# Prompt attention of a hybrid decoder: groups of four tiles formed across block ends, query blocks in alternating order, one VectorE write per group

## The chip, the cores and the metric

The kernel runs on one core of one Trainium2 chip. The metric is the device time of one execution in microseconds (us). Three executions of the kernel before took 3279.99, 3284.44 and 3284.48 us; their median is 3284.44 us.

## What is computed

The program is one inference step of a two-layer decoder for a prompt of 1024 tokens and eight sample tokens that share the weights. Layer 0 is a recurrent block (a gated linear recurrence) with a feed-forward network; layer 1 is sparse attention with a feed-forward network. The change touches only the prompt's attention in layer 1. Its part of the reference is this, with 16 query heads in 4 groups, head width 64 and 1024 query positions in 8 blocks of 128:

```
s_s = einsum(qs, k_g) * scale;  p_s = masked_softmax(s_s, m_s);  o_s = einsum(p_s, v_g)   # selected blocks
s_w = einsum(qs, kw) * scale;   p_w = masked_softmax(s_w, m_w);  o_w = einsum(p_w, vw)    # window of 512
o = g[..., 0:1] * o_c + g[..., 1:2] * o_s + g[..., 2:3] * o_w
```

The compressed branch `o_c` is finished before the stage in question starts; it stands in `oc`, and the other two branches are added to it.

## The kernel before

**Blocks, units and tiles.** A block is one pair of heads (one head in each half of the 128 partitions), given by `r` and `t`, and one query block `i` of 128 positions. `BLOCKS` (L1166) lists 4 x 2 x 8 = 64 of them, and the innermost index is `i` from 0 to 7. Each block has two units, one for each branch `b`: the selected branch reads key tiles 0 to `i`, the window branch key tiles `max(0, i-4)` to `i` (`branch_tiles`, L1169). A tile is 128 queries by 128 keys, for both heads. The eight blocks of one head pair have 2, 4, 6, 8, 10, 11, 12 and 13 tiles, 66 together; the stage has 528 tiles.

**Groups.** Tiles are handled in groups of at most four, since a half of a score bank holds 512 columns. L1185 cuts the tiles of one block into fours, and what is left at the end of a block is a group of its own: a head pair has 1+1+2+2+3+3+3+4 = 19 groups, the stage 152. Of these 112 have four tiles, 8 three, 24 two and 8 one. The rest of the text numbers groups by `g`.

**A ring of scores.** Masked scores are kept in `ring[half]`, 32 tiles each. A unit needs neighbouring places there (`SLOT`), since ScalarE and GpSimd handle a unit in one instruction for each half.

**Steps.** Every engine runs a list written out in the same order of steps `s`. In step `s` group `s` enters and group `s - LAG`, with `LAG` = 5, leaves:

- TensorE (`att_pe`, L1207) transposes the probabilities of group `s-5` (L1235), computes the scores of group `s` (L1220) and multiplies group `s-6` by the values (L1248). Scores have two buffers, so `scores(g)` waits until VectorE has finished the maxima of group `g-2`. `transposes(g)` waits for `p_ready` of the unit to which the last tile of the group belongs. The first `values` of a block waits for `oc_added` of the block two before, which used the same accumulator.
- VectorE (`att_dve`, L1295) does, in this order, a reciprocal for each unit that ended two steps before (L1335), the copy of the transposed upper queries if `s-5` is even (L1323), the addition of a finished block into `oc` (L1329), and `maxima(s)`: for each half a one-element write `dmark` (L1304), then one masked reduction for each run (L1312 with the selection mask, L1315 with the triangular one), each with an accumulator read and a drain. A run is a stretch of tiles of one unit inside a group; the diagonal tile of the selected branch is a run of its own. A run that starts a unit begins from a constant, one that continues a unit begins from the running maximum `nmx`.
- ScalarE (`att_act`, L1267) copies the transposed lower queries of group `s-5` (L1273), for odd groups the upper queries too (L1277), and then takes the exponentials of the units that ended in group `s-1`, one instruction for each half (L1284).
- GpSimd (`att_pool`, L1358) scales each unit by gate and reciprocal, one instruction for each half (L1368), and so sets `p_ready`.

Nothing plans this at run time: the order is fixed by these lists, and the engines meet through semaphores. The sample stage (`smp_pe`, L1386) waits for all 64 `oc_added`; so do the loads of its second sample and later ones.

Of the kernel before, what the change touches and what calls it, by code (L numbers as in the profile page):

```python
# [13 lines left out]
P = 128  # L14
# [70 lines left out]
def build(nc, a, o):  # L85
# [1079 lines left out]

    BLOCKS = [(r, t, i) for r in range(4) for t in range(2) for i in range(QT)]  # L1166
    LAG = 5
# [3 lines left out]

    GROUPS, LAST_GROUP, FIRST_GROUP, UNIT_END, SLOT, EVICTED = [], [], [], [], [], []
    _pos, _owner = 0, [None] * RING
    for _j, (_r, _t, _i) in enumerate(BLOCKS):
        _tiles = []
        for _b in range(2):
            _kt = branch_tiles(_i, _b)
            if _pos + len(_kt) > RING:
                _pos = 0
            SLOT.append(_pos)  # L1180
            _tiles += [(_b, _k, _pos + _n) for _n, _k in enumerate(_kt)]
            _pos += len(_kt)
            UNIT_END.append(None)
        FIRST_GROUP.append(len(GROUPS))
        for _p in range(0, len(_tiles), 4):  # L1185
            _g = _tiles[_p:_p + 4]
            EVICTED.append(max([_owner[_x] + 1 for _, _, _x in _g if _owner[_x] is not None], default=0))
            for _b, _k, _x in _g:
                _owner[_x] = len(GROUPS)
                UNIT_END[2 * _j + _b] = len(GROUPS)  # L1190
            GROUPS.append((_j, _g))
        LAST_GROUP.append(len(GROUPS) - 1)
    NG = len(GROUPS)
    NU = 2 * len(BLOCKS)

    def runs(g, split_diagonal):
        j, tiles = GROUPS[g]
        i = BLOCKS[j][2]
        out = []
        for n, (b, k, x) in enumerate(tiles):  # L1200
            if out and out[-1][0] == b and not (split_diagonal and b == 0 and k == i):
                out[-1][4] += 1
            else:
                out.append([b, k, x, n, 1])
        return out

    def att_pe(pe):  # L1207
# [6 lines left out]
        def scores(g):  # L1214
            r, t, i = BLOCKS[GROUPS[g][0]]
            after(pe, sem("max_done"), 2 * (g - 1))
            for b, k, x, n, w in runs(g, False):
                for half in range(2):
                    hs = slice(64 * half, 64 * half + 64)
                    mm = pe.matmul(PS[half][:, g % 2, n * P:(n + w) * P], QR[hs, r + 4 * t, i * P:(i + 1) * P],  # L1220
                                   KH[b][hs, t, k * P:(k + w) * P], start=True, stop=True, skip_group_check=True)
            mm.then_inc(sem("s_done"), 1)

        def transposes(g):
            j, tiles = GROUPS[g]
            pe.wait_ge(sem("p_ready"), 2 * (2 * j + tiles[-1][0]) + 2)
            after(pe, sem("pt0_ready"), g)
            after(pe, sem("pt_even_ready"), (g + 1) // 2)
            after(pe, sem("pt_odd_ready"), g // 2)
            for half in range(2):  # L1230
                for n, (b, k, x) in enumerate(tiles):
                    for e in range(2):
# [6 lines left out]
        def values(g):  # L1239
            j, tiles = GROUPS[g]  # L1240
            r, t, i = BLOCKS[j]
            if g == FIRST_GROUP[j]:
                after(pe, sem("oc_added"), j - 1)
            pe.wait_ge(sem("pt0_ready"), g + 1)
            pe.wait_ge(sem("pt_odd_ready" if g % 2 else "pt_even_ready"), g // 2 + 1)
            for n, (b, k, x) in enumerate(tiles):
                for half in range(2):
                    mm = pe.matmul(PS[j % 2][64 * half:64 * half + 64, 2, 0:P],  # L1248
                                   VT[b][:, k, t * P + 64 * half:t * P + 64 * half + 64],
                                   pt[g % 2][:, half, n * P:(n + 1) * P], start=(b == 0 and k == 0),  # L1250
                                   stop=(b == 1 and k == i), skip_group_check=True)
# [10 lines left out]
    def half_rows(g, e):  # L1262
        n = len(GROUPS[g][1])
        to = pt[g % 2][:, :, 0:n * P].rearrange("p h (n q) -> p h n q", q=P)[:, :, :, 64 * e:64 * e + 64]
# [30 lines left out]
    def att_dve(dve):  # L1295
        def maxima(g):
            j, tiles = GROUPS[g]
            r, t, i = BLOCKS[j]
            dve.wait_ge(sem("s_done"), g + 1)
            for half in range(2):  # L1300
                if half == 0:
                    after(dve, sem("t0_done"), EVICTED[g])
                    after(dve, sem("t1_done"), EVICTED[g])
                dve.memset(dmark, 0.0)  # L1304
                for b, k, x, n, w in runs(g, True):
                    ps, pb = PS[half][:, g % 2, n * P:(n + w) * P], ring[half][:, x * P:(x + w) * P]
# [18 lines left out]
        def add(j):  # L1325
            r, t, i = BLOCKS[j]
            dve.wait_ge(sem("pv_done"), LAST_GROUP[j] + 1)
            dst = OC[:, r + 4 * t, i * P:(i + 1) * P]
            dve.tensor_tensor(dst, dst, PS[j % 2][:, 2, 0:P], ALU.add).then_inc(sem("oc_added"), 1)  # L1329

        for s in range(NG + LAG + 2):
# [4 lines left out]
            if 0 <= s - LAG < NG and (s - LAG) % 2 == 0:  # L1336
                copy_out(s - LAG)
            if s - LAG - 2 in LAST_GROUP:
                add(LAST_GROUP.index(s - LAG - 2))
            if s < NG:  # L1340
# [1312 lines left out]
```

## Time and profile before

| what | value |
|---|---|
| median of three runs | 3284.44 us (3279.99 to 3284.48) |
| span of the profiled execution | 3282.0 us |
| TensorE busy over the span | 3120.2 us (95%) |
| VectorE busy over the span | 2003.9 us (61%) |
| ScalarE busy | 836.5 us (25%) |
| GpSimd busy | 1187.7 us (36%) |
| prompt attention, first masked reduction to last value matmul | 1706.6 to 2104.6 us |

The profiled execution has a span of 3282.0 us, and the median of the runs is 2.4 us above it. A busy share over the whole span says little here, because TensorE carries the large matrix products of the other stages; what a change in prompt attention is worth is read in its own window of 398 us. "issue" names idle time in which the engine waited for nothing that the profile shows; in this stage such a gap often hides a wait for a semaphore, as can be seen from what the other engines do at that moment.

### The profile page before, as it was taken

To read this page: it belongs to the slowest core of one execution; us is meant where nothing else is said; L and a number is where in the kernel's file an instruction comes from. 1 tells how busy PE (TensorE), PEld (TensorE's weight loads), DVE (VectorE), ACT (ScalarE), POOL (GpSimd) and SP (SyncE) were. 2 spreads that over 40 slices of the span, in tenths; PEclk is the share of its full clock that TensorE was granted. 3 is DMA by queue.
4 is the path that set the end of the run, shared out by engine and by line. 5 is a ranking of instruction groups with operands and counts; after the bars stand their busy time and mean duration, and the time that the engine had idled before them with its cause. 6 is when DMAs were issued, how large, how long until landed. Compare 5 with 4: busy or idle time off the path is not lost.

```text
span 3282.0 us, 57052 instructions
## 1 busy us (share of the span) xinstructions
PE 3120.2 (95%) x22560; PEld 2835.1 (86%) x22560; DVE 2003.9 (61%) x3712; ACT 836.5 (25%) x1404; POOL 1187.7 (36%) x801
## 2 busy tenths in 40 slices
PE   6999999999999999999889999998999999999996
PEld 4988989999999998999656666675989999999996
DVE  4567286657475676764468888501259567585776
ACT  4555131101010102110237777400231101010001
POOL 1332424444434443334025555300424444444441
PEclk8999999999999999999869999999999999999998
DMA  5223322122121112321662000274221111111112
GB/s 201 83 67 102 127 102 91 65 72 83 59 96 52 65 46 94 130 78 39 206 213 104 2 2 2 74 243 159 103 96 40 51 46 46 46 46 47 51 46 113
DMA packets 78015, 277.89 MB, mean 85 GB/s; under 512 B 8858, under 2 KB 19362, under 8 KB 74546
## 3 DMA queue, kind: packets, MB, share of 16 engines
q1 hardware_dynamic: 75202, 256.83, 23.0%
q10 hardware_dynamic: 2576, 17.73, 1.6%
q8 instruction: 170, 2.79, 0.3%
q14 instruction: 67, 0.55, 0.1%
HBM read 247.54 MB, written 36.27 MB: 86 GB/s over the span
## 4 chain that ended last, share of the span: by engine, by line
PE 76%; DVE 10%; issue 7%; ACT 3%; DVEq 2%; DMA 1%; SPq 0%; POOL 0%; POOLq 0%; ACTq 0%
PE PB L2008 32%; PE PA L2008 30%; PE PB L1413 3%; DVE ring L1315 3%; DVE ring L1312 1%; PE PA L2044 1%; PE PA L1382 1%; PE PB L2044 1%; ACT ring L1284 1%; DVEq L1316 1%; DMA mw<-in_mw 1%; PE PC L284 1%; DVE pt L1323 1%; PE PC L1235 1%; PE PB L1452 0%
## 5 line engine op out<-in xcount | busy, mean ns | idle before, releaser
L1780 POOL TENSOR_TENSOR w_hi<-w_raw,misc 128x1024 fp32r<-128x1024 f32 x192 | 378.1, 1969 | 1535.5 <-PE PA L2008 635.8
L1782 POOL TENSOR_TENSOR w_lo<-w_raw,w_hi 128x1024 fp32r<-128x1024 f32 x192 | 560.3, 2918 | 27.3
L2008 PE MATMUL PA<-hB_hi,w_hi 128*128 128x348 f32 x1272 | 274.1, 324 | 0.0
L2008 PE MATMUL PB<-hB_hi,w_hi 128*128 128x348 f32 x1272 | 272.3, 322 | 0.0
L2008 PE MATMUL PA<-hB_hi,w_lo 128*128 128x348 f32 x1272 | 271.6, 322 | 0.0
L2008 PE MATMUL PB<-hB_hi,w_lo 128*128 128x348 f32 x1272 | 271.5, 322 | 0.0
L2008 PE MATMUL PA<-hB_lo,w_hi 128*128 128x348 f32 x1272 | 271.2, 321 | 0.0
L2008 PE MATMUL PB<-hB_lo,w_hi 128*128 128x348 f32 x1272 | 271.0, 321 | 0.0
L2008 PEld LDWEIGHTS PA<-hB_lo,w_hi 128*128 128x128 f32 x1272 | 215.4, 188 | 0.0
L2008 PEld LDWEIGHTS PB<-hB_hi,w_hi 128*128 128x128 f32 x1272 | 214.9, 188 | 0.4
L2008 PEld LDWEIGHTS PB<-hB_lo,w_hi 128*128 128x128 f32 x1272 | 215.1, 188 | 0.0
L2008 PEld LDWEIGHTS PA<-hB_hi,w_hi 128*128 128x128 f32 x1272 | 214.4, 188 | 0.4
L2008 PEld LDWEIGHTS PA<-hB_hi,w_lo 128*128 128x128 f32 x1272 | 214.4, 188 | 0.0
L2008 PEld LDWEIGHTS PB<-hB_hi,w_lo 128*128 128x128 f32 x1272 | 214.1, 188 | 0.0
L1368 POOL TENSOR_SCALAR ring<-ring,gtok,psm 128x640 f32<-128x640 f32 (+7 forms) x256 | 196.5, 772 | 0.1
L1284 ACT ACTIVATE ring<-ring,nmx 128x640 f32<-128x640 f32 (+7 forms) x256 | 185.8, 731 | 11.4 <-DVE nmx L1315 10.4
L486 DVE TENSOR_TENSOR ua<-ua,rms 128x1032 f32<-128x1032 f32 x48 | 114.3, 2382 | 67.5 <-ACT ua L424 67.2
L486 DVE TENSOR_TENSOR ub<-ub,rms 128x1032 f32<-128x1032 f32 x46 | 85.9, 1867 | 86.0 <-ACT ub L424 86.0
L1235 PEld LDWEIGHTS PC<-ident,ring 64*128 64x128 f32 x1056 | 77.3, 138 | 64.8 <-issue 43.7
L374 DVE TENSOR_TENSOR t<-t,sq 128x1032 f32<-128x1032 f32 x28 | 48.7, 1738 | 136.4 <-ACT sq L368 135.1
L537 DVE TENSOR_TENSOR O<-O,PB 128x1032 f32<-128x1032 f32 x40 | 49.1, 1228 | 134.0 <-PE PB L2008 133.2
L1235 PE MATMUL PC<-ident,ring 64*128 64x64 f32 x1056 | 96.3, 228 | 34.5 <-DVE pt L1323 26.2
(640 smaller groups left out, 6897.5 us busy)
## 6 DMA issues: line engine op xcount, KB each, us to landing
w_raw<-in_w SPq DMA_DIRECT2D x196, 512.0 KB, 3.6
mt<-in_mw SPq DMA_DIRECT2D x32, 1024.0 KB, 5.0
pages<-in_pages SPq DMA_DIRECT2D x64, 384.0 KB, 4.2
x_dram<-X SPq DMA_DIRECT2D x12, 1032.0 KB, 4.0
X<-x_dram SPq DMA_DIRECT2D x3, 4128.0 KB, 12.4
mw<-in_mw SPq DMA_DIRECT2D x4, 2048.0 KB, 22.8
mt_even<-in_mw SPq DMA_DIRECT2D x8, 1024.0 KB, 5.0
mt_odd<-in_mw SPq DMA_DIRECT2D x8, 1024.0 KB, 5.4
```

What stands on the lines that cost most here:

```text
L374: dve.tensor_tensor(acc, acc, sq_of(n, k), ALU.add).then_inc(sem("acc_added"), 1)
L486: dve.tensor_tensor(u[:, 2:2 + TOK], u[:, 2:2 + TOK], rms, ALU.mult)
L537: dve.tensor_tensor(dst, dst, ps, ALU.add).then_inc(sem("sum_out"), 1)
L1235: mm = pe.transpose(PCD[e][:, c:c + 64], ring[half][q, x * P:(x + 1) * P], ident[q, q])
L1284: act.activation(p, p, ACT.Exp, bias=nmx[:, u % 16, half:half + 1], scale=-1.0, accum_out=psm[:, u % 16, half:half + 1]).then_inc(sem("exp ...
L1315: mx = dve.tensor_tensor_reduce(pb, ps, wmask[:, c0:c0 + w * P], -SCALE, first, ALU.add, ALU.min, nm)
L1368: pool.tensor_scalar(p, p, gtok[:, i, gate:gate + 1], psm[:, u % 16, half:half + 1], ALU.mult, ALU.mult).then_inc(sem("p_ready"), 1)
L1413: mm = pe.matmul(dst.rearrange("p g (j b) -> p j g b", b=8), (sw1k if kv == 0 else sw1v)[:, m, :], rhs, start=(m == 0), stop=(m == 15), sk ...
L1780: pool.tensor_tensor(hi, raw, zero.broadcast_to([P, 1024]), ALU.add)
L1782: pool.tensor_tensor(lo, raw, hi.bitcast(F32), ALU.subtract).then_inc(sem("w_split"), 1)
L2008: mm = pe.matmul(PS[ps][:, c, 0:width], w[:, w0:w0 + P], x[:, k, c * width:(c + 1) * width], start=(k == 0 and n == 0), stop=(k == K - 1 a ...
L2044: mm = pe.matmul(PS[(p0 + b) % 2][:, c, 0:CW], w[(t + b) % 2][:, k * P:(k + 1) * P], x[:, k, c * CW:(c + 1) * CW], start=(first and i == 0 ...
```

## The change

Three things change in prompt attention.

1. The order of the eight query blocks inside a head pair is 7, 3, 6, 2, 5, 1, 4, 0 in place of 0 to 7.
2. The tiles of all blocks are put in one list and cut into fours, so a group may hold the end of one block and the start of the next: 132 groups, all of four tiles. `GROUPS`, `UNIT_END`, `LAST_GROUP` and `EVICTED` are worked out for it, and `runs` keeps the block beside the branch. `values` now waits for `oc_added` in every group, for the block two before the one of the group's last tile, which may have ended in the group just before.
3. The one-element write `dmark` is made once in a group in place of once for each half.

```diff
--- before.py
+++ after.py
@@ -1163,46 +1163,43 @@
             act.dma_start(QR[64 * h:64 * h + 16, 4 * t:4 * t + 4, :],
                           q_dram[2][t * P:(t + 1) * P].rearrange("(n h d) c -> h d n c", h=2, d=16)[h]).then_inc(sem("q_back"), 16)
 
-    BLOCKS = [(r, t, i) for r in range(4) for t in range(2) for i in range(QT)]
+    BLOCKS = [(r, t, i) for r in range(4) for t in range(2) for i in (7, 3, 6, 2, 5, 1, 4, 0)]
     LAG = 5
 
     def branch_tiles(i, b):
         return list(range(0 if b == 0 else max(0, i - 4), i + 1))
 
-    GROUPS, LAST_GROUP, FIRST_GROUP, UNIT_END, SLOT, EVICTED = [], [], [], [], [], []
-    _pos, _owner = 0, [None] * RING
+    TILES, UNIT_END, SLOT = [], [], []
+    _pos = 0
     for _j, (_r, _t, _i) in enumerate(BLOCKS):
-        _tiles = []
         for _b in range(2):
             _kt = branch_tiles(_i, _b)
             if _pos + len(_kt) > RING:
                 _pos = 0
             SLOT.append(_pos)
-            _tiles += [(_b, _k, _pos + _n) for _n, _k in enumerate(_kt)]
+            TILES += [(_j, _b, _k, _pos + _n) for _n, _k in enumerate(_kt)]
             _pos += len(_kt)
-            UNIT_END.append(None)
-        FIRST_GROUP.append(len(GROUPS))
-        for _p in range(0, len(_tiles), 4):
-            _g = _tiles[_p:_p + 4]
-            EVICTED.append(max([_owner[_x] + 1 for _, _, _x in _g if _owner[_x] is not None], default=0))
-            for _b, _k, _x in _g:
-                _owner[_x] = len(GROUPS)
-                UNIT_END[2 * _j + _b] = len(GROUPS)
-            GROUPS.append((_j, _g))
-        LAST_GROUP.append(len(GROUPS) - 1)
+            UNIT_END.append((len(TILES) - 1) // 4)
+    GROUPS = [TILES[_p:_p + 4] for _p in range(0, len(TILES), 4)]
     NG = len(GROUPS)
     NU = 2 * len(BLOCKS)
+    LAST_GROUP = [max(g for g in range(NG) if any(_tile[0] == _j for _tile in GROUPS[g])) for _j in range(len(BLOCKS))]
+    EVICTED, _owner = [], {}
+    for _g, _tiles in enumerate(GROUPS):
+        EVICTED.append(max([_owner[_x] + 1 for _, _, _, _x in _tiles if _x in _owner], default=0))
+        _owner.update((_x, _g) for _, _, _, _x in _tiles)
 
     def runs(g, split_diagonal):
-        j, tiles = GROUPS[g]
-        i = BLOCKS[j][2]
         out = []
-        for n, (b, k, x) in enumerate(tiles):
-            if out and out[-1][0] == b and not (split_diagonal and b == 0 and k == i):
-                out[-1][4] += 1
+        for n, (j, b, k, x) in enumerate(GROUPS[g]):
+            if out and out[-1][:2] == [j, b] and not (split_diagonal and b == 0 and k == BLOCKS[j][2]):
+                out[-1][5] += 1
             else:
-                out.append([b, k, x, n, 1])
+                out.append([j, b, k, x, n, 1])
         return out
+
+    def out_place(j):
+        return PS[j % 2][:, 2, 0:P]
 
     def att_pe(pe):
         pe.wait_ge(sem("sc_read"), 16)
@@ -1212,9 +1209,9 @@
         pe.wait_ge(sem("q_back"), 16 * 4)
 
         def scores(g):
-            r, t, i = BLOCKS[GROUPS[g][0]]
             after(pe, sem("max_done"), 2 * (g - 1))
-            for b, k, x, n, w in runs(g, False):
+            for j, b, k, x, n, w in runs(g, False):
+                r, t, i = BLOCKS[j]
                 for half in range(2):
                     hs = slice(64 * half, 64 * half + 64)
                     mm = pe.matmul(PS[half][:, g % 2, n * P:(n + w) * P], QR[hs, r + 4 * t, i * P:(i + 1) * P],
@@ -1222,13 +1219,13 @@
             mm.then_inc(sem("s_done"), 1)
 
         def transposes(g):
-            j, tiles = GROUPS[g]
-            pe.wait_ge(sem("p_ready"), 2 * (2 * j + tiles[-1][0]) + 2)
+            tiles = GROUPS[g]
+            pe.wait_ge(sem("p_ready"), 2 * (2 * tiles[-1][0] + tiles[-1][1]) + 2)
             after(pe, sem("pt0_ready"), g)
             after(pe, sem("pt_even_ready"), (g + 1) // 2)
             after(pe, sem("pt_odd_ready"), g // 2)
             for half in range(2):
-                for n, (b, k, x) in enumerate(tiles):
+                for n, (j, b, k, x) in enumerate(tiles):
                     for e in range(2):
                         q = slice(64 * e, 64 * e + 64)
                         c = half * 256 + n * 64
@@ -1237,15 +1234,14 @@
                             mm.then_inc(sem(f"t{e}_done"), 1)
 
         def values(g):
-            j, tiles = GROUPS[g]
-            r, t, i = BLOCKS[j]
-            if g == FIRST_GROUP[j]:
-                after(pe, sem("oc_added"), j - 1)
+            tiles = GROUPS[g]
+            after(pe, sem("oc_added"), tiles[-1][0] - 1)
             pe.wait_ge(sem("pt0_ready"), g + 1)
             pe.wait_ge(sem("pt_odd_ready" if g % 2 else "pt_even_ready"), g // 2 + 1)
-            for n, (b, k, x) in enumerate(tiles):
+            for n, (j, b, k, x) in enumerate(tiles):
+                r, t, i = BLOCKS[j]
                 for half in range(2):
-                    mm = pe.matmul(PS[j % 2][64 * half:64 * half + 64, 2, 0:P],
+                    mm = pe.matmul(out_place(j)[64 * half:64 * half + 64, :],
                                    VT[b][:, k, t * P + 64 * half:t * P + 64 * half + 64],
                                    pt[g % 2][:, half, n * P:(n + 1) * P], start=(b == 0 and k == 0),
                                    stop=(b == 1 and k == i), skip_group_check=True)
@@ -1260,7 +1256,7 @@
                 values(s - LAG - 1)
 
     def half_rows(g, e):
-        n = len(GROUPS[g][1])
+        n = len(GROUPS[g])
         to = pt[g % 2][:, :, 0:n * P].rearrange("p h (n q) -> p h n q", q=P)[:, :, :, 64 * e:64 * e + 64]
         return to, PCD[e].rearrange("p (h n q) -> p h n q", h=2, q=64)[:, :, 0:n, :]
 
@@ -1294,15 +1290,13 @@
 
     def att_dve(dve):
         def maxima(g):
-            j, tiles = GROUPS[g]
-            r, t, i = BLOCKS[j]
             dve.wait_ge(sem("s_done"), g + 1)
+            after(dve, sem("t0_done"), EVICTED[g])
+            after(dve, sem("t1_done"), EVICTED[g])
+            dve.memset(dmark, 0.0)
             for half in range(2):
-                if half == 0:
-                    after(dve, sem("t0_done"), EVICTED[g])
-                    after(dve, sem("t1_done"), EVICTED[g])
-                dve.memset(dmark, 0.0)
-                for b, k, x, n, w in runs(g, True):
+                for j, b, k, x, n, w in runs(g, True):
+                    r, t, i = BLOCKS[j]
                     ps, pb = PS[half][:, g % 2, n * P:(n + w) * P], ring[half][:, x * P:(x + w) * P]
                     nm = nmx[:, (2 * j + b) % 16, half:half + 1]
                     first = 3e38 if k == branch_tiles(i, b)[0] else nm
@@ -1326,7 +1320,7 @@
             r, t, i = BLOCKS[j]
             dve.wait_ge(sem("pv_done"), LAST_GROUP[j] + 1)
             dst = OC[:, r + 4 * t, i * P:(i + 1) * P]
-            dve.tensor_tensor(dst, dst, PS[j % 2][:, 2, 0:P], ALU.add).then_inc(sem("oc_added"), 1)
+            dve.tensor_tensor(dst, dst, out_place(j), ALU.add).then_inc(sem("oc_added"), 1)
 
         for s in range(NG + LAG + 2):
             for u in range(NU):
@@ -1335,8 +1329,9 @@
                     dve.reciprocal(psm[:, u % 16, :], psm[:, u % 16, :]).then_inc(sem("sum_inverted"), 1)
             if 0 <= s - LAG < NG and (s - LAG) % 2 == 0:
                 copy_out(s - LAG)
-            if s - LAG - 2 in LAST_GROUP:
-                add(LAST_GROUP.index(s - LAG - 2))
+            for j in range(len(BLOCKS)):
+                if LAST_GROUP[j] == s - LAG - 2:
+                    add(j)
             if s < NG:
                 maxima(s)
         dve.drain()
```

## Rows read from the trace of the kernel before

**Rows 1.** The page's 40 equal slices, tenths busy: TensorE and VectorE.

```profile
PE   6999999999999999999889999998999999999996
...
DVE  4567286657475676764468888501259567585776
```

**Rows 2.** Busy time by stage: prompt attention and its tail. Columns: window, length, engines, clock, DMA.

```profile
1706.60:2095.30 388.70, 349.39 (x4886) 237.04 (x4884) 313.39 (x1559) 291.17 (x729) 215.65 (x381) 0.99 0.11 39
2095.30:2104.60 9.30, 7.69 (x137) 6.36 (x133) 1.95 (x5) 6.35 (x13) 2.75 (x4) 1.00 0.01 4
```

**Rows 3.** Waits in 1720 to 2090 us: waiter, releaser, total us, times, longest.

```profile
PE PC L1235 <- DVE pt L1323: 23.7, 37, 1.6
PEld PC L1235 <- POOL ring L1368: 17.8, 31, 2.2
...
DVE ring L1312 <- issue: 7.4, 16, 1.2
DVE psm L1335 <- ACT ring L1284: 6.4, 17, 0.8
...
PEld PA L1248 <- DVE oc L1329: 2.3, 3, 0.8
...
DVE pt L1323 <- PE PA L1248: 0.2, 1, 0.2
```

**Rows 4.** Timeline of VectorE: start us, duration us, instruction.

```profile
1843.02 0.69 DVE L1323 COPY pt<-PD 128x512 f32<-128x512 f32 x1
1843.63 0.28 DVE L1329 TENSOR_TENSOR oc<-oc,PA 128x128 f32<-128x128 f32 x1
1843.84 0.69 DVE L1312 CUSTOM_DVE_ANT_1 ring<-PA,selm 128x512 f32<-128x512 f32 x1
...
1844.44 0.08 DVE L1312 DVE_READ_ACCUMULATOR2_ANT nmx<- 128x1 f32 x1
1844.64 0.06 DVE L1304 MEMSET misc<- 1x1 f32 x1
1844.70 0.69 DVE L1312 CUSTOM_DVE_ANT_1 ring<-PB,selm 128x512 f32<-128x512 f32 x1
...
1853.40 0.29 DVE L1315 CUSTOM_DVE_ANT_0 ring<-PB,wmask 128x128 f32<-128x128 f32 x1
...
1853.81 0.29 DVE L1315 CUSTOM_DVE_ANT_0 ring<-PB,wmask 128x128 f32<-128x128 f32 x1
...
1857.28 0.35 DVE L1315 CUSTOM_DVE_ANT_0 ring<-PB,wmask,nmx 128x128 f32<-128x128 f32 x1
1857.56 0.08 DVE L1315 DVE_READ_ACCUMULATOR2_ANT nmx<- 128x1 f32 x1
1857.76 0.42 DVE L1315 CUSTOM_DVE_ANT_0 ring<-PB,wmask 128x256 f32<-128x256 f32 x1
```

**Rows 5.** Timeline of TensorE, one round of a full group.

```profile
1990.52 0.65 PE L1220 MATMUL PA<-k_sel,xq 64*128 64x512 f32 x1
...
1991.53 0.66 PE L1248 MATMUL PB<-pt,v_sel 128*64 128x128 f32 x8
...
1992.55 0.27 PE L1235 MATMUL PC<-ident,ring 64*128 64x64 f32 x1
...
1993.10 0.65 PE L1220 MATMUL PA<-k_win,xq 64*128 64x512 f32 x1
```

**Rows 6.** Timeline of ScalarE, VectorE and GpSimd after an eight-tile unit.

```profile
2092.11 1.15 ACT L1284 ACTIVATE ring<-ring,nmx 128x1024 f32<-128x1024 f32 x1
...
2093.38 0.17 DVE L1335 RECIPROCAL psm<-psm 128x2 f32<-128x2 f32 x1 [0.81 <-ACT ring L1284]
...
2093.80 1.18 POOL L1368 TENSOR_SCALAR ring<-ring,gtok,psm 128x1024 f32<-128x1024 f32 x1
```

**Rows 7.** Timeline: a TensorE wait and the VectorE wait behind it.

```profile
1813.60 0.29 PE L1235 MATMUL PC<-ident,ring 64*128 64x64 f32 x1 [1.98 <-POOL ring L1368]
...
1815.92 0.55 DVE L1312 CUSTOM_DVE_ANT_1 ring<-PA,selm 128x384 f32<-128x384 f32 x1 [1.24 <-issue]
```

## The prediction, made before the changed kernel was run

> **What bounds the kernel now.** I first looked for the stage in the 40 slices of the page: VectorE stands at 8 tenths for four slices on end only in the middle, TensorE at 9 nearly everywhere [rows 1]. The middle is prompt attention. The busy time by stage then gives its size: VectorE 313.4 us and TensorE 349.4 us of 388.7 us, and behind the last maxima a tail of 9.3 us [rows 2]. By busy time TensorE would be the bound. The waits say otherwise: TensorE stands 23.7 us for VectorE's copy and 17.8 us for GpSimd's scaled tiles, while VectorE has ten entries from 7.4 down to 0.2 us, 77 gaps and 24.9 us together [rows 3]. Some 0.05 us of each gap is ordinary sequencing, so VectorE idles about 24.9 - 77 x 0.05 = 21 us. Its work is 388.7 - 21 = 368 us, more than its 313 busy us, because each reduction is followed by an accumulator read and a drain that the page does not count: from 1857.56 to 1857.76 only 0.08 us are busy [rows 4]. That is 368/152 = 2.42 us for a group.
>
> TensorE's own round for a full group runs 1.01 us from scores to values, 1.02 to the transposes, 0.55 to the next scores: 2.58 us [rows 5]. A round of full groups on VectorE must be compared with that. So VectorE sets the end, with TensorE close behind, and the stage's time is VectorE's work, plus its idle time, plus start and tail. The next stage waits for the last addition, so what is gained or lost here goes to the end whole; the same is true of little else, since weight loads elsewhere are untouched.
>
> **Part 1, the cut into groups.** Tiles stay 528, so all work by columns stays. What changes is the number of instructions. Counting from the code, a half has 248 runs before: 128 that start a unit and 120 that continue one. After, it has 272: again 128, and 144. So there are 24 x 2 = 48 more continuing reductions. A one-tile reduction from a constant takes 1853.40 to 1853.81, 0.41 us; one from the running maximum 1857.28 to 1857.76, 0.48 us; a four-tile one 0.80 us to the next start [rows 4]. A tile is therefore (0.80 - 0.41)/3 = 0.13 us, and the fixed part 0.28 or 0.35 us. Since the columns only move, the added price is 48 x 0.35 = **+16.8 us**; with the other fixed part it would be +13.4. I take the first, because every added run continues a unit.
>
> VectorE's copies of even groups fall from 76 to 66. A four-tile copy takes 1843.02 to 1843.63, 0.61 us [rows 4], of which 4 x 0.13 is columns: 10 x 0.09 = **-0.9 us**. Reciprocals (128) and additions (64) stay. On TensorE the full groups cost 132 x 2.58 = 341 us, below VectorE's work, and its 28 more score runs for a half lie in that slack. ScalarE makes 30 fewer copies, off the path. The cost of all this, if the cover goes, stands with the rivals.
>
> The Trainium skill speaks against the new cut: VectorE: DVE Perf Modes, The TRN2 errata, holds that a fixed latency is paid by each instruction, so many small operands cost more than a large one, and its Rules for kernel authors say "Minimize op *count*, not sems". By its 120 cycles for an operand in PSUM, an estimate is 48 x 0.125 = 6 us, and the sum would then be 10.8 us lower, -6.7 us. The trace's fixed part of 0.28 to 0.35 us, which holds the accumulator read and the drain too, decides against that figure.
>
> **Part 2, one write less.** 304 writes become 132. In the second half of each of the 152 groups the write is exposed: an accumulator read to the next reduction is 0.26 us with it (1844.44 to 1844.70) and 0.20 us without (1857.56 to 1857.76) [rows 4]. The times are given to 0.01, so I take 0.055 us for each: 152 x 0.055 = **-8.4 us**. The bounds are 0, if the drain fills the gap anyway, and 9.1 at 0.06. The 20 first-half writes that go with their groups mostly lie in the shadow of a copy or an addition (1843.63 to 1843.84 leaves no place for more), between 0 and -1.1: **-0.5 us**.
>
> VectorE's work so changes by 16.8 - 0.9 - 8.4 - 0.5 = **+7.0 us**, to about 375, or 2.84 us a group. That is 0.26 above TensorE's round.
>
> **Part 3, order and waits: what happens to the 21 us of idle time.** Before, I find it mainly in two places. One is the stretch of small blocks, where five steps are short: at 1813.60 TensorE has stood 1.98 us for GpSimd, and VectorE pays for it with 1.24 us at 1815.92 [rows 7]. The other is behind long units: after the exponentials of eight tiles (1.15 us a half) the reciprocal came 0.81 us late [rows 6]. Since every group is now full, the first kind goes; about 15 us of the 21. What is late next:
>
> - *Exponentials*. A unit of seven tiles can end where ScalarE has an odd group to copy: two copies, then 2 x 1.03 us (1.15 less a tile). The next group is a single run for each half, 2 x (0.80 + 0.07) = 1.7 us. I find four such places among the 33 groups of a round of 16 blocks, 0.85, 0.7, 0.55 and 0.45 us late: 2.55 us, and 10.2 in four rounds. (By the same reckoning the old kernel has 6.2.)
> - *A unit over three groups*. Before, the last tile's unit ends at most one group later, now two groups later at 12 groups. Then the reciprocal comes one step before the transposes. GpSimd takes 2 x 1.18 us for eight tiles [rows 6] and 0.2 of its own, the transposes 0.55, the scores 1.01: over 4 us against one VectorE step and the start of the next. At 12 places 0.3 to 0.9 us, 7 us together.
> - *The accumulator*. `values` now waits for an addition that VectorE makes at the start of the same step, at 15 groups (before, the group that ended lay at least two back). Behind the waiting matmul stand the transposes and the next scores. When it goes, TensorE owes 1.02 + 0.55 + 1.01 and some 0.2 of signals, 2.8 us, and VectorE has only this group's maxima to cover it, 1.75 us where it is one run a half. About 0.35 us a place, 5.4 us. Rows of before show this wait only three times, 2.3 us [rows 3].
>
> Together 22.6 us; a place that is late for two reasons pays once, so I take 18, which is 3 less than before. The bounds are 6 (only part of the exponentials show) and 32 (second rival).
>
> The start is 0.6 us later, since the first group has four tiles' scores to wait for and not two, and the tail, whose last units now have one tile, is put 0.5 us shorter; it stays bound by TensorE's last five groups.
>
> **Sum.** 7.0 - 3.0 + 0.6 - 0.5 = +4.1 us. On the profiled span of 3282.0 that is 3286.1 us. The median of the runs is 2.4 above the span, so 3288.5 us. A measurement of this kernel can tell about 0.2%, 6.6 us, from no change; the forecast lies within it.
>
> **The rivals.**
>
> *The idle time all but goes (faster).* Full groups and alternating lengths keep each engine supplied, and the late places cover each other. For it: TensorE's round is constant and shorter than VectorE's mean, and with two score buffers a short step is paid for only when two come together. Against it: the 0.81 us behind exponentials has not to do with group sizes. Idle 6 us: 7.0 - 15 = -8.0, 3276.4 us.
>
> *TensorE loses its lead (slower).* It is one mechanism: at 27 groups (12 and 15 above) TensorE cannot run ahead of VectorE, since it waits within a round for something that VectorE makes at the round's start or one before. The place is `transposes` or `values` of these groups, and the next scores come late. If each costs 0.8 us, two thirds of the 1.24 seen in rows 7, that is 21.6, with 10.2 from the exponentials 31.8 us of idle time: 7.0 + 10.8 = +17.8, 3302.2 us. My forecast has about 7.8 us left at these 27, 0.29 each; from 0.39 each the result passes 6.6 us and is slower. Against it: most of these groups stand beside long maxima.
>
> *The write was free.* If it filled a drain's gap, its removal gives nothing and the change does not do what its third part says: 4.1 + 8.9 = +13.0, 3297.4 us. Against it stands the 0.06 us between two gaps of the same kind.
>
> **How the numbers follow.** Forecast 0.43, with its own range of 3280 to 3292; idle time gone 0.27; lead lost 0.25; write free 0.05. Faster by over 0.2% is 0.27, slower by over 0.2% is 0.25 + 0.05 = 0.30, within is 0.43. The range takes the first rival with 3 us for its bounds, 3273, and the second whole, 3303.
>
> **What would show it.** After: 544 reductions where 496 were, 132 writes at L1304's place, the gap from accumulator read to the second half's first reduction at 0.20 us. VectorE's busy time in the stage rises by some 10 us (48 x 0.44 for reduction and read, less 172 writes of 0.06). TensorE's waits for GpSimd's ring and for `oc` should be the ones that grow; "DVE psm <- ACT" should be near 10 us. I am wrong if VectorE's idle time is far from 18 us, or if the fixed part of a continuing reduction is not 0.34 us. If TensorE's round were the bound after all, the stage would follow 132 x 2.58 and reductions would cost nothing.

## The result, and the profile after

The changed kernel took 3291.49 us (median of 7 runs, 3286.95 to 3294.77); the kernel before, run with it, 3282.12 us (7 runs). The ratio is 1.003 with a 95% interval of 1.002 to 1.0041: slower by 9.4 us. Four more runs of it in a later session gave a ratio of 1.0041 (1.0026 to 1.0056). I had forecast 3288.5 us, +4.1 on the profiled span, in a range of 3273 to 3303, with 0.43 for no measurable change and 0.30 for slower.

The page of the changed kernel in 40 slices; read it against [rows 1]. VectorE shows 7 tenths where it showed 8, TensorE 8 where it showed 9:

```profile
PE   6999999999999999999878888898999999999996
...
DVE  4666276657475676754577777501259577585776
...
PEclk8999999999999999999889999999999999999998
```

Both engines are *less* busy by share, which means that the stage has become longer, not that there is less to do. The stage itself, from the first masked reduction to the last maxima, and the tail behind it (columns as in [rows 2]):

```profile
1699.60:2099.40 399.80, 346.11 (x5004) 249.06 (x5002) 315.37 (x1469) 287.42 (x694) 212.10 (x372) 0.97 0.11 38
2099.40:2111.60 12.20, 8.92 (x137) 7.40 (x132) 2.89 (x11) 7.05 (x19) 5.85 (x12) 0.86 0.01 2
```

The stage went from 388.7 to 399.8 us and the tail from 9.3 to 12.2. VectorE's busy time is hardly up (313.4 to 315.4 us): 48 more reductions with their reads are paid for in part by 172 writes less, and the drain behind each is not in this column. So I took the sum apart from the start times. VectorE's instructions follow each other at fixed distances when nothing is late (0.20 us from an accumulator read to the next reduction, 0.61 us from a four-tile copy, and so on); what a gap has above its usual length by more than 0.06 us I call idle, the rest work. What is taken as usual can move about 1 us between the two columns, so differences of idle time under 1 us say nothing; the stage's length does not depend on it. By this count, with the stage ending at the last addition:

| kernel | reductions | VectorE's work | idle | tail | stage |
|---|---|---|---|---|---|
| before | 496 | 366.6 | 22.0 | 9.2 | 397.7 |
| changed | 544 | 377.1 | 22.6 | 12.1 | 411.9 |
| changed, second profile | 544 | 377.3 | 21.9 | 12.0 | 411.2 |

All in us. The stage is 14.2 us longer: 10.5 us of work and 2.9 of tail, with idle time unchanged (0.6). The second profile repeats it within 1 us. The profiled span grew by only 6.4 us (3282.0 to 3288.4), since in this execution the stage began 7.05 us earlier, at 1699.66 us and not 1706.71. The code ahead of it is the same; the granted clock there differs between executions. The 50 us ahead of the stage, first before, then changed:

```profile
1650.00:1700.00 50.00, 45.09 (x248) 27.31 (x240) 31.77 (x128) 14.13 (x30) 6.29 (x10) 0.63 0.56 179
```

```profile
1650.00:1700.00 50.00, 38.95 (x269) 23.61 (x267) 33.60 (x137) 15.72 (x32) 6.39 (x10) 0.83 0.69 210
```

0.63 and 0.83 of full speed. Over all profiles of the study the stage's start lies between 1697.9 and 1706.9 us, without order by kernel (1699.7 and 1702.8 for the changed one). The medians, over more executions, are the better measure of the whole kernel: +9.4 and, in the later session, +13.7 us (3293.35 to 3279.66).

The waits of the changed kernel in the same window as [rows 3]:

```profile
PEld PC L1232 <- POOL ring L1363: 30.5, 30, 2.8
...
PEld PB L1244 <- DVE oc L1323: 20.3, 14, 2.3
...
PE PC L1232 <- POOL ring L1363: 23.4, 13, 2.6
...
PE PB L1244 <- DVE oc L1323: 11.3, 12, 1.6
...
PE PC L1232 <- DVE pt L1317: 9.2, 16, 1.2
...
DVE psm L1329 <- ACT ring L1280: 2.2, 4, 0.7
```

TensorE stands for GpSimd's ring for 30.5 and 23.4 us (weight loads and matmuls; 17.8 and 7.7 before), for the accumulator in PB 20.3 and 11.3 us (0.3 before; PA had the 2.3 of [rows 3]). The wait for VectorE's copy fell from 23.7 to 9.2, and VectorE's wait for ScalarE's exponentials from 6.4 to 2.2 us.

### The profile page after: what moved, and what is told of

The parts are those of the page before. It is cut to its first block, busy times and chain, and to the rows that moved or that the text cites. A ratio compares the mean times of both kernels' runs of the same rounds, so it can differ in the third digit from the quotient of the medians.

```text
span 3288.4 us, 57100 instructions
## 1 busy us (share of the span) xinstructions
PE 3104.3 (94%) x22672; PEld 2838.5 (86%) x22672; DVE 2006.5 (61%) x3626; ACT 832.9 (25%) x1374; POOL 1187.2 (36%) x801
## 4 chain that ended last, share of the span: by engine, by line
PE 75%; issue 9%; DVE 6%; POOL 4%; DVEq 2%; ACT 2%; POOLq 1%; DMA 1%; SPq 0%; ACTq 0%
PE PB L2003 32%; PE PA L2003 30%; POOL ring L1363 4%; PE PB L1408 3%; PE PA L2039 1%; PE PB L2039 1%; PE PA L1377 1%; POOLq L1365 1%; PE PC L284 1%; DMA mw<-in_mw 1%; DVE ring L1309 1%; DVE ring L1306 1%; PE PB L1447 0%; DVE t L2304 0%; PE PC L2047 0%
```

## Experiments

All stages below are read as in the table above. Times are medians with the ratio to the kernel before of the same session.

### One write less, alone

```diff
                 if half == 0:
                     after(dve, sem("t0_done"), EVICTED[g])
                     after(dve, sem("t1_done"), EVICTED[g])
-                dve.memset(dmark, 0.0)
+                    dve.memset(dmark, 0.0)
```

> The kernel before with one thing changed: the one-element write stands once in a group, before the first half only. Theory (VectorE's work sets the stage, and the profile after shows a gap of 0.22 us where 0.25 us were): VectorE's work falls by 152 x 0.03 = 4.6 us from 366.6 us, idle time stays near 22 us, time -4 to -5 us. Rival 1 (my prediction's price, 0.055 us each): -8.4 us. Rival 2 (TensorE's round is the bound): 0.

Measured: 3275.89 us, ratio 0.9982 (0.9973 to 0.9992). Work 361.6 us, idle 21.0, stage 391.7: 5.0 us of work and 1.0 of idle time less. Its stage without the tail:

```profile
1705.50:2088.10 382.60, 347.35 (x4884) 235.90 (x4883) 304.84 (x1407) 290.55 (x729) 216.38 (x381) 0.99 0.11 39
```

The price of a write is 5.0/152 = 0.033 us, not 0.055, so rival 1 is wrong, and a stage that follows VectorE's work rules out rival 2. The reason can be read in the changed kernel's timeline. Between two reductions of one half the read is followed by the next reduction after 0.20 us; across the halves, where the write has gone, after 0.22 us:

```profile
1866.93 0.08 DVE L1306 DVE_READ_ACCUMULATOR2_ANT nmx<- 128x1 f32 x1
1867.13 0.35 DVE L1309 CUSTOM_DVE_ANT_0 ring<-PA,wmask,nmx 128x128 f32<-128x128 f32 x1
...
1867.96 0.08 DVE L1309 DVE_READ_ACCUMULATOR2_ANT nmx<- 128x1 f32 x1
1868.18 0.35 DVE L1306 CUSTOM_DVE_ANT_1 ring<-PB,selm,nmx 128x128 f32<-128x128 f32 x1
```

With the write the gap across the halves is 0.25 us in most groups (0.26 in [rows 4]); without it 0.22 us, which is still 0.02 us longer than the gap inside a half. I had compared 0.26 with the inner 0.20, so I priced the write and a part that stays.

### The order alone

```diff
-    BLOCKS = [(r, t, i) for r in range(4) for t in range(2) for i in range(QT)]
+    BLOCKS = [(r, t, i) for r in range(4) for t in range(2) for i in (7, 3, 6, 2, 5, 1, 4, 0)]
```

> The kernel before with the block order 7, 3, 6, 2, 5, 1, 4, 0 alone: groups still end with their block (152 groups, 496 reductions, two writes). Theory: VectorE's work stays at 366.6 us within 1; of the idle time of 22 us the part that came from the stretch of small blocks goes (1.26 us at one place in a round, 5 us in all), the tail grows by 0 to 3 us because four groups now follow in short order behind the last long unit: time -4 to +1 us. Rival (the order itself makes TensorE lose its lead, through the accumulator wait): idle grows, time +3 us or more.

Measured: 3278.94 us, ratio 0.9991 (0.9982 to 1.0001). Work 366.6, idle 18.8, stage 394.2 us. The order gives 3.5 us in the stage; the interval of the time reaches to no change. The rival, that it costs TensorE's lead, is wrong here. With one write as well:

> The kernel before with the new block order and one write in a group, groups still ending with their block. Theory: the two add up, work 361.6 us, idle 18.8 us, tail 9 us: stage 389 us, time -9 us against the kernel before (6.0 for the write, 3.5 for the order, by the stages of the two single runs). Rival (both gain from the same idle time): -6 us, no better than the one write alone.

Measured: 3275.21 us, ratio 0.9987 (0.9978 to 0.9997); work 361.0, idle 20.5, stage 390.4 us. That is 7.3 us less than before where 9 were expected, and 1.3 less than with one write alone: the gains overlap, and the rival is nearer the truth.

### The cut across block ends: with two writes, and in the old order

```diff
-            dve.memset(dmark, 0.0)
             for half in range(2):
+                dve.memset(dmark, 0.0)
```

> The changed kernel with the second write put back (one before each half). Theory: VectorE's work 377.1 + 132 x 0.03 = 381 us, time +4 us against the changed kernel. Rival (the changed stage is set by TensorE's waits for the accumulator and for GpSimd, not by VectorE's work): idle takes it up, time within 1 us of the changed kernel.

Measured: 3299.39 us, ratio 1.0053 (1.0036 to 1.007), against 3291.49 for the changed kernel. Work 381.7 us, 4.6 more than changed (4.0 expected); but idle rose too, 22.6 to 26.7, and the stage is 420.4 us. So VectorE's work is paid in full, and idle time does not take it up. It even grew: behind the three-group units of the section on the idle time it went from 11.9 to 15.2 us. The mean granted clock over the stage, 0.96 where the changed kernel has 0.97, points at the effect of the last section, but how much of the growth is due to it is not shown.

> The changed kernel with the blocks in order 0 to 7 again: 132 groups across block ends, one write, 528 reductions in place of 544 (272 in place of 288 continue a unit). Theory: VectorE's work is 16 x 0.344 = 5.5 us less than in the changed kernel, 371.6 us; the tail is the old one, 9.2 and not 12.1 us; idle 22 us: stage 403 us, time -8 us against the changed kernel and +5 against the one before. Rival (idle time from the accumulator and three-group units decides; 11 groups with the accumulator wait, not 15, and the small blocks in a row again): idle above 28 us, time no better than the changed kernel.

Measured: 3297.9 us, ratio 1.0051 (1.0034 to 1.0067). Work was as expected, 370.9 us; idle 30.0 us and a tail of 11.9 were not: stage 412.9 us. The rival was right about the idle time, and the tail belongs to the cut and not to the order. Against the kernel with one write (391.7 us), which differs from this one in the cut alone, the cut costs 21.2 us: 9.3 of work, 9.0 of idle time, 2.8 of tail. In the new order it costs 411.9 - 390.4 = 21.5 us.

### The price of a reduction

```diff
-            if out and out[-1][0] == b and not (split_diagonal and b == 0 and k == i):
+            if out and out[-1][0] == b and not (split_diagonal and (n == 2 or b == 0 and k == i)):
```

> The kernel before with each run that reaches over the middle of its group cut in two there: 88 more reductions in each half, 176 in all, all continuing a unit, the same columns and the same groups. Theory (VectorE sets the stage, a continuing reduction costs 0.34 us beside its columns): work 366.6 + 60 = 427 us, and since longer steps cover the other engines, idle time falls from 22 to 5 to 10 us: stage +43 to +48 us, time the same. Rival (TensorE's round of 2.58 us is nearly the bound, much of VectorE's time is slack): less than +30 us. Rival (a fixed cost of 0.125 us, as for one access to PSUM): work +22 us.

Measured: 3336.52 us, ratio 1.0179 (1.0163 to 1.0196), +56.8 us. Work 427.6 us, so 61.0/176 = 0.347 us for each added reduction; idle 17.5 us (5 to 10 expected); stage 454.6 us. The stage, without the tail, with TensorE busy for 360 of 445 us:

```profile
1697.80:2142.90 445.10, 359.58 (x4883) 244.27 (x4882) 352.72 (x1911) 298.61 (x729) 215.17 (x381) 0.97 0.09 34
```

That VectorE bounds the stage, and the 0.35 us, are shown by this. By the Trainium skill's figure of 120 cycles, 0.125 us, for an operation whose input is in PSUM, as the scores are (VectorE: DVE Perf Modes, The TRN2 errata) an estimate would be 22 us; the measured 61.0 us decides against it for a reduction with accumulator read and drain.

### Where the idle time of the cut comes from

In the changed kernel I laid each late start of VectorE beside the group it belongs to. Of 22.6 us, 11.9 lie behind the 12 groups whose last unit ends two groups later, 4.7 behind the 15 groups with the accumulator wait, 2.0 in front of four reciprocals, and the rest is spread over many small gaps. First the lag:

```diff
-    LAG = 5
+    LAG = 6
```

> The changed kernel with the lag between a group's scores and its transposes raised from 5 to 6 steps; nothing else. Theory (a unit that spreads over three groups has too little time between its reciprocal and its transposes: in the profile after, 11.9 us of VectorE's 22.6 us of idle time lie behind these 12 groups): this idle time goes, work stays at 377 us, the tail grows by one round of TensorE without scores (1.02 + 0.55 = 1.6 us): stage 412 - 12 + 2 = 402 us, time -8 to -10 us against the changed kernel. Rival (the accumulator wait is what holds TensorE at these groups): idle stays above 18 us, time within 3 us.

Measured: 3283.13 us, ratio 1.0013 (1.0003 to 1.0022). Work 377.3, idle 9.6, stage 399.2 us (402 expected). Next to nothing of the idle time is left behind three-group units. TensorE's waits:

```profile
PE PC L1232 <- DVE pt L1317: 23.9, 34, 1.8
PEld PB L1244 <- DVE oc L1323: 14.6, 12, 2.2
...
PEld PC L1232 <- POOL ring L1363: 8.9, 21, 1.7
...
PE PC L1232 <- POOL ring L1363: 2.5, 3, 1.0
```

The waits for GpSimd fell from 54 to 11 us. The waits for the accumulator hardly fell (41 to 38 us, PA and PB, weight loads and matmuls). Behind them VectorE still has four late starts of 0.3 to 1.0 us, 3 us together where there were 4.7: most of these waits are covered, not all. The mean granted clock over the stage rose from 0.97 to 0.99.

Then the accumulator wait, made shorter by an addition half a step earlier:

```diff
                 mx.then_inc(sem("max_done"), 1)
+                if half == 0:
+                    for j in between:
+                        add(j)
...
-            for j in range(len(BLOCKS)):
-                if LAST_GROUP[j] == s - LAG - 2:
-                    add(j)
+            ended = [j for j in range(len(BLOCKS)) if LAST_GROUP[j] == s - LAG - 1]
             if s < NG:
-                maxima(s)
+                maxima(s, ended)
```

> The changed kernel with the addition of a finished block into oc made half a step earlier: between the two halves of the maxima of the step before, not at the start of the step. The wait of the values for oc_added stays. Theory: TensorE's listed waits for oc (20 + 11 + 6 + 3.5 us) fall below half, but VectorE's idle time falls only by the 4.7 us that lie behind the 15 groups with no group between, since the rest is covered; VectorE itself may now wait for the values in a few steps (below 2 us): time -2 to -5 us. Rival (lead lost at these groups is the main cost of the change): -10 us or more.

Measured: 3301.04 us, ratio 1.0068 (1.0051 to 1.0084), no gain; stage 414.2 us. Its waits:

```profile
PEld PC L1232 <- POOL ring L1367: 38.4, 28, 3.3
PE PC L1232 <- POOL ring L1367: 32.3, 19, 3.1
...
PEld PA L1244 <- DVE oc L1326: 6.8, 9, 0.8
...
PEld PB L1244 <- DVE oc L1326: 5.1, 7, 0.8
```

The waits for `oc` are down to 12 us and the idle time behind these groups to 0.4 us, as both theories had it. But idle behind the three-group units rose from 11.9 to 18.7 us, and TensorE's waits for GpSimd from 54 to 71. What was taken away at one place came back at the other: TensorE arrives earlier at `transposes` and stands there. The wait alone does not make the loss, though. At group 16 of the second and the fourth round of 33 groups it stood 1.3 us before the transposes in the changed kernel and 3.05 and 3.06 us here. These are the 3 us ahead of the maxima that follow, first in the changed kernel, then here; the last number but two is the granted clock:

```profile
1857.60:1860.60 3.00, 1.71 (x26) 1.32 (x28) 2.04 (x12) 1.22 (x4) 1.42 (x4) 1.00 0.01 3
2059.70:2062.70 3.00, 1.73 (x28) 1.35 (x30) 1.96 (x13) 1.23 (x5) 1.63 (x4) 1.00 0.00 0
```

```profile
1863.70:1866.70 3.00, 2.37 (x26) 1.58 (x28) 1.40 (x8) 1.62 (x4) 1.62 (x4) 0.73 0.01 3
2067.00:2070.00 3.00, 1.69 (x26) 1.30 (x28) 1.77 (x11) 0.94 (x2) 1.82 (x4) 1.00 0.00 0
```

VectorE started 0.5 us late in both rounds of the changed kernel. Here it started 0.7 us late in the fourth round, where the clock stayed at 1.00, and 1.4 us late in the second, at 0.73, after the same wait. So a large part of what came back at this place is scores at a lower clock; the last section has the same effect in the changed kernel. My expectation of -2 to -5 us was wrong, and the rival's -10 more so.

### The lag with the other kernels

> The kernel before with one write in a group and the lag raised from 5 to 6. Theory: of the 21 us of idle time the 5.5 us in front of reciprocals (they wait for ScalarE, whose distance is fixed at two steps) stay, of the other 15.5 us half goes, since transposes have a step more in the short steps of the small blocks; tail +1 us: stage 391.7 - 7 + 1 = 386 us, time -6 us against the one write alone, -12 against the kernel before. Rival (without units over three groups the lag is long enough already): idle stays at 21 us, the tail is 1 us longer, time +1 us.

Measured: 3273.91 us, ratio 0.9983 (0.9974 to 0.9992); stage 391.9 us, idle 20.0. The lag gives nothing to the old groups (391.7 with lag 5): the rival holds. With the new order too:

> The same with the new block order as well: groups end with their block, one write, lag 6. Theory: as for the order in place before, idle 20.5 us falls by some 7 us, tail +1: stage 384 us, time -13 us against the kernel before. Rival: the lag gives nothing here, 391 us.

3275.62 us, ratio 0.999 (0.9981 to 0.9999), idle 17.8, stage 390.1 us: again nothing.

> Groups across block ends with the blocks in order 0 to 7, one write, lag 6. Theory (the time is the sum of work, idle time and tail, and the lag takes the idle time behind units over three groups): work 371 us as with lag 5, idle from 30 to 10 us, tail 12.5: stage 394 us, time -18 us against lag 5 and still no better than the old groups with one write (391.7 us), because 32 more reductions are left. Rival (part of the idle time of the ascending order comes from the small blocks and stays): idle 20 us, stage 404 us.

Measured: 3278.3 us, ratio 0.9997 (0.9988 to 1.0006). Work 369.7, idle 10.1, stage 393.0 us, where the sum of the three terms had given 394. Its stage and tail:

```profile
1702.50:2082.40 379.90, 338.47 (x4917) 241.28 (x4914) 309.53 (x1437) 287.00 (x699) 213.58 (x378) 0.99 0.10 37
2082.40:2095.70 13.30, 11.16 (x177) 9.46 (x177) 3.19 (x10) 7.05 (x13) 4.43 (x6) 0.87 0.02 4
```

This is the cut at its best, and it only draws level with the old groups and one write (391.7 us): what its fuller groups save in idle time goes on 32 more reductions and on the tail.

> The changed kernel once more, for a second profile. Theory: the stage repeats within 2 us of 411.9 us (work 377, idle 23, tail 12), and what differs between profiled executions lies before the stage, where the granted clock changes between executions: the stage's start may move by some us. Rival: the stage itself varies by 5 us or more, so that single profiles can't carry the sums.

Measured: 3293.35 us, ratio 1.0041; the stage repeated at 411.2 us.

**The best kernels** are the ones with one write alone (3275.89 us, ratio 0.9982) and the same with lag 6 (3273.91, 0.9983). They beat both the kernel before and the changed one; between them no difference shows, nor clearly from the two with the new order as well (0.9987 and 0.999).

## Why the prediction was right or wrong

- **What bounds the stage.** Right. The stage follows VectorE's work: +61.0 us by the split gave +56.9 in the stage, -5.0 by the write -6.0. It does so less exactly in the new order, where one write took 5.6 us of work and 3.8 of the stage (394.2 to 390.4).
- **Part 1, +16.8 us for 48 reductions.** Right in mechanism and size: the split measured 0.347 us each, the sum took 0.35. Between the two kernels with one write and the new order the work differs by 377.1 - 361.0 = 16.1 us; with the copies' 0.9 us added back, 17.0/48 = 0.354.
- **Part 2, -8.4 us for the write.** The term was mis-sized: 5.0 us over the 152 groups. The bounds of 0 and 9.1 held it. Together the work rose by 10.5 and not 7.0 us. The sign that I gave for it, VectorE's busy time up by some 10 us, failed too (it rose by 2.0): 0.44 us for a reduction and its read holds a tile's columns, which only move.
- **Part 3, idle time from 21 to 18 us.** Measured 22.6. It fell as expected in the small-block stretch, and the list of late places was right in kind but not in size. Units over three groups: 7 forecast, 11.9 measured (9.6 in the second profile). Accumulator: 5.4 forecast, 4.7 measured. Exponentials: 10.2 forecast, 2.0 measured: the step failed. The waits show 2.2 us, four times, where I had said near 10. I had found four places in a round and multiplied by four rounds. But ScalarE has its second copy at odd groups, and with 33 groups in a round a place that is odd in one round is even in the next. A reciprocal behind a seven-tile unit was late in the second and the fourth round only:

```profile
1818.69 0.17 DVE L1329 RECIPROCAL psm<-psm 128x2 f32<-128x2 f32 x1 [0.69 <-ACT ring L1280]
2020.14 0.17 DVE L1329 RECIPROCAL psm<-psm 128x2 f32<-128x2 f32 x1 [0.69 <-ACT ring L1280]
```

  One more, of 0.6 us at 1899.54, follows three units that end together. Why ScalarE was early at the other places no run parts. The discount from the added-up 22.6 to 18 us had no working behind it; that the measured idle time is 22.6 as well is chance, since the terms behind the sum are off in both directions.
- **The tail, -0.5 us.** Wrong, +2.9 us. The last five groups hold 20 tiles and not 17, and the last group holds the ends of three units. In the changed kernel's timeline the upper half of a group is copied only after three reciprocals, which wait for three pairs of exponentials, and TensorE stands for that copy:

```profile
2099.70 1.72 POOL L1363 TENSOR_SCALAR ring<-ring,gtok,psm 128x640 f32<-128x640 f32 x2
...
2101.95 0.17 DVE L1329 RECIPROCAL psm<-psm 128x2 f32<-128x2 f32 x1 [0.60 <-ACT ring L1280]
2102.03 0.69 DVE L1317 COPY pt<-PD 128x512 f32<-128x512 f32 x1
...
2102.98 0.34 PE L1232 MATMUL PC<-ident,ring 64*128 64x64 f32 x1 [2.33 <-DVE pt L1317]
```

  That wait is 2.33 us. I had looked for copies queued behind waits in the steps and not in the tail. In the ascending order, whose last group ends a single unit, the tail is 11.9 us all the same, so the three units can't be the whole cause. The three more tiles are the other candidate: with the new order and the old groups the last five groups hold 16 tiles, and the tail is 8.8 us. No run parts the two.
- **The sum.** +4.1 forecast, +9.4 measured and +14.2 in the stage of one profile. Of the 10.1 us between forecast and stage, 3.5 are work (3.4 of them the write), 3.6 idle time and 3.4 the tail; 0.6 goes off for a start that I had added and that this count does not hold. The time itself, 3288.5 forecast and 3291.49 measured, looks nearer than the change was: I had started from a median of 3284.44 us over three executions, and over seven it is 3282.12. And the profiled span, 3288.4 with 3286.1 forecast, is near only by luck, since this execution's stage began 7.05 us earlier than the one before. The change of +9.4 us lies above the 6.6 us within which I had put 0.43; the result is the slower case, at 0.30.
- **The rivals.** *Idle time all but goes* was wrong at lag 5, and is nearly what lag 6 does (9.6 us). *TensorE loses its lead* was right in its place, the 27 groups, with 16.6 us of idle time behind them and not 21.6; it was the side on which the result fell. From 0.39 us each I had said it decides; it was 16.6/27 = 0.61. What the rival did not hold is that part of this loss is the granted clock (last section). *The write was free* was wrong.
- With the price of 0.125 us from the Trainium skill (VectorE: DVE Perf Modes, The TRN2 errata) the sum would have been -6.7 us, an estimate of the wrong sign for this kernel.

## What to carry to other kernels

Fuller groups are worth only what the fixed cost of a group is, and here that was small (one copy's 0.09 us), while each cut of a group inside a unit costs the engine that bounds the stage a whole reduction, 0.35 us. Before packing work across boundaries, count the bounding engine's instructions and not the groups. A lag that is counted in groups must cover the longest unit in groups: when packing made a unit's last tiles lie two groups ahead of its end and not one, the lag had to grow by one too. And when one wait is shortened, look at where the freed engine stands next, and at the granted clock there.

## What the hardware showed beyond this

The same place can cost 1.0 or 2.3 us, and the granted clock decides which. Groups 9, 42, 75 and 108 hold the window tiles of block 2 and the first tile of block 5, whose unit ends two groups later. In the second of the four rounds TensorE stood 2.58 us for GpSimd there, and VectorE's next scores came late:

```profile
1834.07 0.18 POOL L1359 TENSOR_TENSOR misc<-misc 1x1 f32<-1x1 f32 x1 [3.93 <-DVE psm L1329]
...
1836.22 0.27 PE L1232 MATMUL PC<-ident,ring 64*128 64x64 f32 x1 [2.58 <-POOL ring L1363]
...
1836.83 0.18 POOL L1359 TENSOR_TENSOR misc<-misc 1x1 f32<-1x1 f32 x1 [0.66 <-DVE psm L1329]
...
1838.95 0.48 DVE L1306 CUSTOM_DVE_ANT_1 ring<-PA,selm,nmx 128x256 f32<-128x256 f32 x1 [1.11 <-issue]
```

Two-microsecond stretches around it, last but two column the granted clock:

```profile
1834.00:1836.00 2.00, 0.00 (x0) 0.00 (x0) 1.32 (x7) 1.67 (x6) 1.93 (x3) 1.00 0.02 4
1836.00:1838.00 2.00, 1.78 (x20) 1.44 (x22) 1.35 (x5) 0.89 (x2) 1.34 (x4) 0.65 0.00 0
1838.00:1840.00 2.00, 2.00 (x18) 1.51 (x16) 0.85 (x5) 0.69 (x4) 1.84 (x4) 0.50 0.00 0
```

It falls from full to half speed after that wait, though TensorE is busy for 346 of the stage's 400 us, and the score matmul of 384 columns at 1836.87 us takes 0.95 us where the one at 1818.20 took 0.48. So a wait of TensorE can be followed by slower scores, and VectorE then pays for both. In the second profile of the same kernel the four rounds of this place:

```profile
1733.00:1745.00 12.00, 9.85 (x138) 7.67 (x138) 7.85 (x41) 8.14 (x21) 7.14 (x13) 0.86 0.70 280
1834.00:1846.00 12.00, 9.41 (x126) 7.25 (x124) 8.29 (x40) 7.80 (x20) 7.08 (x14) 0.86 0.01 2
1935.00:1947.00 12.00, 9.18 (x139) 6.67 (x134) 8.84 (x46) 9.52 (x25) 6.72 (x13) 1.00 0.01 3
2036.00:2048.00 12.00, 8.54 (x132) 6.29 (x128) 9.22 (x47) 9.40 (x25) 6.31 (x12) 1.00 0.01 1
```

At a clock of 0.86 in these 12 us VectorE lost 2.35 and 1.74 us at the place, at 1.00 it lost 1.05 and 1.00. In the first profile it was the second, third and fourth round that ran at half speed here, with 1.66, 2.35 and 2.31 us lost, and the first, at full speed, that lost 1.06. TensorE's wait was as long at either clock: 2.15 and 2.58 us in the second profile's first two rounds, 2.36 and 2.58 in its last two. So it is the clock that makes the difference; why it fell in some rounds and not in others no run shows. Of the 2.3 us between 11.9 and 9.6 us of idle time behind three-group units in the two profiles, these four places hold 1.2.

The Trainium skill (TensorE: Matmul & The Clock Gate, What's actually happening) gives the two levels, 1.2 and 2.4 GHz, and the lower one to an idle engine. The trace agrees in the levels (0.50 and 1.00) and in that the falls shown follow idle time of TensorE; it does not show one after each such wait.

The kernel before has the effect too, at the place of [rows 7]: after the wait of 1.98 us its clock is 0.50 in 1815 to 1817 us, and a score matmul of 512 columns takes 1.16 us where [rows 5] has 0.65. The 1.24 us that I read there as the price of a wait holds the price of a lower clock. The lower clock is not what made the tail longer: with lag 6 the tail ran at 1.00 and took 12.3 us.
